# Weight sums of a paired feed-forward product made by accumulating DMAs from GpSimd, in a two-layer encoder trunk

## The reference, cut to what matters

```
for i in range(2):
    u = rms_norm(h, mix_norm_g[i])
    h = h + (conv_pool_mixer if i == 0 else gla_mixer)(u, ...)
    u = rms_norm(h, ffn_norm_g[i])
    a = relu(u @ ffn_w1[i])            # (528, 1024) @ (1024, 4096)
    h = h + (a * a) @ ffn_w2[i]        # (528, 4096) @ (4096, 1024)
return rms_norm(h[:, 16:], final_norm_g)
```

## Time and profile before

| | |
|---|---|
| median of 3 runs | 1162.88 us |
| profiled execution | 1161.42 us |
| its span | 1159.6 us |
| granted TensorE clock | 0.995 |
| TensorE busy | 1127.1 us, 97% |
| VectorE busy | 753.5 us, 65% |
| ScalarE busy | 522.0 us, 45% |
| GpSimd busy | 2.3 us |
| HBM traffic | 99.1 MB, 85 GB/s over the span |

### The profile page before, as it was taken

The page is one execution under the profiler, slowest core; times in us unless marked ns, Lnnn a source line. Parts: engine busy times, 40 slices in busy tenths (PEclk is TensorE's granted clock), DMA queues, the critical chain, the costliest instruction groups (busy, mean ns, idle before and its releaser), DMA issues.

```text
span 1159.6 us, 19207 instructions
## 1 busy us (share of the span) xinstructions
PE 1127.1 (97%) x7817; PEld 1048.7 (90%) x7817; DVE 753.5 (65%) x1039; ACT 522.0 (45%) x802; POOL 2.3 (0%) x30
## 2 busy tenths in 40 slices
PE   6999999999999999999999999999989999999997
PEld 6999999999999999999999888787889899899886
DVE  5898897786686785454353345665786786785443
ACT  7436554454454444333443133543454444454332
POOL 0000000000000000000000000000000000000000
PEclk9999999999999999999899999999999999999999
DMA  6322022233233224222113211132224224224311
GB/s 200 109 73 73 2 73 73 73 109 110 74 105 114 72 76 141 87 96 73 56 56 109 73 45 64 38 109 73 73 73 146 73 76 142 72 81 136 109 37 73
DMA packets 98819, 100.10 MB, mean 86 GB/s; under 512 B 2786, under 2 KB 95644, under 8 KB 98748
## 3 DMA queue, kind: packets, MB, share of 16 engines
q1 hardware_dynamic: 98684, 99.02, 26.5%
q10 hardware_dynamic: 64, 0.07, 0.0%
HBM read 96.99 MB, written 2.10 MB: 85 GB/s over the span
## 4 chain that ended last, share of the span: by engine, by line
PE 86%; DVE 6%; ACT 4%; issue 2%; DMA 1%; SPq 0%; ACTq 0%; DVEq 0%
PE ps L1701 53%; PE ps L1888 19%; PE ps L1955 5%; PE ps L1817 3%; PE ps L1997 1%; PE ps L2012 1%; DVE relu L1359 1%; PE ps L1749 1%; PE ps L1709 1%; DVE w_lo L494 1%; DVE c_lo L1378 1%; DMA raw<-in_cp_w_in_dram 1%; ACT parts L879 1%; ACT w_hi L487 1%; DVE rstd L1155 1%
## 5 line engine op out<-in xcount | busy, mean ns | idle before, releaser
L1701 PE MATMUL ps<-u_lo,w_hi 128*128 128x272 f32 (+1 forms) x1120 | 298.9, 323 | 3.3 <-DVE u_lo L1197 3.3
L1701 PE MATMUL ps<-u_hi,w_hi 128*128 128x272 f32 (+1 forms) x1120 | 295.6, 319 | 0.0
L1701 PE MATMUL ps<-u_hi,w_lo 128*128 128x272 f32 (+1 forms) x1120 | 295.2, 319 | 0.0
L494 DVE TENSOR_TENSOR w_lo<-raw,w_hi 128x1024 fp32r<-128x1024 f32 x132 | 161.1, 1223 | 117.9 <-ACT w_hi L487 117.9
L487 ACT ACTIVATE w_hi<-raw 128x1024 fp32r<-128x1024 f32 x132 | 138.4, 1052 | 146.5 <-PE ps L1701 135.4
L1701 PEld LDWEIGHTS ps<-u_lo,w_hi 128*128 128x128 f32 x1120 | 183.8, 188 | 21.4 <-issue 6.3
L1888 PE MATMUL ps<-c_lo,w_hi 128*128 128x264 f32 (+1 forms) x672 | 190.5, 284 | 11.9 <-ACT ps L902 9.1
L1701 PEld LDWEIGHTS ps<-u_hi,w_hi 128*128 128x128 f32 x1120 | 184.6, 189 | 16.2 <-issue 1.2
L1701 PEld LDWEIGHTS ps<-u_hi,w_lo 128*128 128x128 f32 x1120 | 183.6, 188 | 15.3
L1888 PE MATMUL ps<-c_hi,w_lo 128*128 128x264 f32 (+1 forms) x672 | 189.9, 283 | 0.0
L1888 PE MATMUL ps<-c_hi,w_hi 128*128 128x264 f32 (+1 forms) x672 | 189.7, 282 | 0.0
(11 more groups left out here) (241 smaller groups left out, 1545.8 us busy)
## 6 DMA issues: line engine op xcount, KB each, us to landing
raw<-in_ffn_w_dram SPq DMA_DIRECT2D x64, 1024.0 KB, 5.4
raw<-in_gla_w_in_dram SPq DMA_DIRECT2D x12, 1024.0 KB, 5.3
raw<-in_cp_w_in_dram SPq DMA_DIRECT2D x8, 512.0 KB, 5.3
raw<-in_cp_w_out_dram SPq DMA_DIRECT2D x4, 1024.0 KB, 5.1
raw<-in_gla_w_out_dram SPq DMA_DIRECT2D x4, 1024.0 KB, 5.1
xin<-in_x_dram SPq DMA_DIRECT2D x4, 512.0 KB, 5.4
raw<-in_cp_w_in_dram SPq DMA_DIRECT2D x2, 1024.0 KB, 5.1
out_dram<-y_tok SPq DMA_DIRECT2D x4, 512.0 KB, 3.0
```

Source lines behind the costliest of these rows:

```text
L494: dve.tensor_tensor(w_view(w_lo, n), half_view(raw, n), w_view(w_hi, n).bitcast(F32), ALU.subtract).then_inc(w_lo_ready, 1)
L1701: last = mm(ps[:, n % NS, c:c + b - a], l, r[:, a - origin:b - origin], start=(k == 0 and i == 0), stop=(k == count - 1 and i == 2))
```

## The change

The sums of weights are no longer made by VectorE. For each pair SP loads four tiles of `s_sum` straight from `ffn_w2`, GpSimd adds three more quarters by accumulating DMAs, waits, and adds s1 into s2 and s4 by two more. ScalarE's `pair_hi` waits for the last of these. To have only additions, all signs are positive: S1 = A21 + A22, S2 = A11 + S1, S3 = A11 + A21, S4 = A11 + A12 + S1; T1 is E1 - E2, the others change sign to suit, the kept copy of y is taken times -1, and the second row of outputs is subtracted from `h`.

The order in steps `i` changes: the weight group of an even step 4 or 6 comes behind the parts E1 to T1; the parts T2 to O2 are split in two (T2 alone, then O1 and O2), which makes four part groups per step pair instead of three; and pair 0's seed copy stands between them in step 7. The hardware loop is gone: all three blocks are written out, and `it` with it.

```diff
+        def w2_unit(layer, fb, p, m, k):
+            w2 = ffn_w2[layer].rearrange("(k p) n -> p k n", p=P)
+            at = 2 * P * p + P * m
+            return w2[:, fb * KD + k:(fb + 1) * KD:2, at:at + P]
 @ pair_hi
             if g in (1, 2):
-                act.wait_ge(s_ready, 4 * pair_number(layer, fb, p) + g + 2 + 16 * it)
+                act.wait_ge(sum_ready, 32 * (pair_number(layer, fb, p) + 1))
 @ sync
+            def load_sums(layer, fb, p):
+                b = pair_raw(layer, fb, p)
+                if p:
+                    sp.wait_ge(w_lo_ready, GROUPS[b - 1] + 3)
+                elif fb or layer:
+                    sp.wait_ge(w_lo_ready, GROUPS[pair_raw(layer, fb - 1, 3) if fb else pair_raw(0, PAIRED - 1, 3)] + 3)
+                for i, (m, k) in enumerate(((1, 0), (0, 0), (0, 0), (0, 0))):
+                    sp.dma_start(s_sum[:, i, :, :], w2_unit(layer, fb, p, m, k)).then_inc(sum_loaded, 16)
                     for j in range(4):
                         load(b + 4 + j, w2[:, fb * KD:(fb + 1) * KD, 256 * j:256 * (j + 1)])
+                        if fb < PAIRED:
+                            load_sums(layer, fb, j)
 @ gpsimd
+            def add_sums(layer, fb, p):
+                q = pair_number(layer, fb, p)
+                s1, s2, s3, s4 = (s_sum[:, i, :, :] for i in range(4))
+                pool.wait_ge(sum_loaded, 64 * (q + 1))
+                for dst, m, k in ((s1, 1, 1), (s4, 0, 1), (s3, 1, 0)):
+                    pool.dma_start(dst, w2_unit(layer, fb, p, m, k), accum_op=ALU.add).then_inc(sum_first, 16)
+                pool.wait_ge(sum_first, 48 * (q + 1))
+                for dst in (s2, s4):
+                    pool.dma_start(dst, s1, accum_op=ALU.add).then_inc(sum_ready, 16)
 @ scalar, step i
-                            pair_hi(layer, fb, 0, i - KD // 2, it)
-                        act.wait_ge(t_ready, 3 * count + 1 + 12 * it)
-                        act.activation(c_hi[:, E1:T1 + 1, j, 0:w], now[:, E1:T1 + 1, :], ACT.Copy)
+                        part_hi(E1, T1, 1)
+                        if i >= KD // 2:
+                            pair_hi(layer, fb, 0, i - KD // 2)
 ...
+                        part_hi(T2, T2, 2)
+                        if i == KD - 1:
+                            seed(0)
+                        part_hi(O1, O2, 2)
+                        part_hi(T3, T4, 3)
 @ vector, pair p
-                    if p < KD // 2 - 1:
-                        pair_sums(layer, fb, p + 1, it)
-                    dve.wait_ge(copied, 2 * q + 2 + 8 * it)
+                    dve.wait_ge(copied, 2 * q + 2)
 @ scalar, vector, tensor
-                paired_ffn(layer, 0, tokens)
-                with act.Fori(0, FBLK - 2) as it:
-                    paired_ffn(layer, 1, tokens, it)
+                for fb in range(PAIRED):
+                    paired_ffn(layer, fb, tokens)
```

More of the change, by code:

```diff
@@ L664, in _ @@
             last.then_inc(consts, 3)
+            def add_sums(layer, fb, p):
[7 more added lines that the diff above has]
+                    pool.dma_start(dst, s1, accum_op=ALU.add).then_inc(sum_ready, 16)
+            for layer in range(2):
+                for fb in range(PAIRED):
+                    for p in range(KD // 2):
+                        add_sums(layer, fb, p)
         @block.scalar
@@ L864, in paired_ffn, with part_hi @@
                     now = parts8[:, j % 2, :, 0:w]
-                    evacuated(act, n, it)
+                    evacuated(act, n)
                     src = relu[:, i % 2, a:b].rearrange("p (t n) -> p t n", t=2)
+                    def part_hi(first, last, t):
+                        act.wait_ge(t_ready, 3 * count + t)
+                        act.activation(c_hi[:, first:last + 1, j, 0:w], now[:, first:last + 1, :], ACT.Copy)\
+                           .then_inc(part_hi_ready, 1)
                     if i % 2 == 0:
@@ L876, in paired_ffn @@
[L876 to L877 removed]
+                            split_hi(block + i + 4)
+                        part_hi(E1, T1, 1)
+                        if i >= KD // 2:
+                            pair_hi(layer, fb, 0, i - KD // 2)
                     else:
                         act.activation(now[:, O1:O2 + 1, :], src, ACT.Square).then_inc(sq_ready, 1)
[L880 removed]
@@ L1392, in paired_ffn @@
                          .then_inc(t_ready, 1)
                         part_lo(E1, T1, 1)
-                    else:
-                        dve.wait_ge(sq_ready, t + 1 + 8 * it)
-                        V.tensor_tensor(now[:, T2, :], now[:, O2, :], now[:, T1, :], ALU.subtract)\
+                        if i >= KD // 2:
+                            pair_lo(layer, fb, 0, i - KD // 2)
+                    else:
+                        dve.wait_ge(sq_ready, t + 1)
+                        V.scalar_tensor_tensor(out=now[:, T2, :], in0=now[:, T1, :], scalar=-1.0,
+                                               in1=now[:, O2, :], op0=ALU.mult, op1=ALU.subtract)\
@@ L1397, in paired_ffn @@
                          .then_inc(t_ready, 1)
                         V.tensor_tensor(now[:, T3, :], now[:, O2, :], now[:, E2, :], ALU.subtract)
-                        dve.wait_ge(t_ready, 3 * count + 2 + 12 * it)
-                        V.tensor_tensor(now[:, T4, :], now[:, O1, :], now[:, T2, :], ALU.subtract)\
+                        part_lo(T2, T2, 2)
+                        dve.wait_ge(t_ready, 3 * count + 2)
+                        V.scalar_tensor_tensor(out=now[:, T4, :], in0=now[:, T2, :], scalar=-1.0,
+                                               in1=now[:, O1, :], op0=ALU.mult, op1=ALU.subtract)\
@@ L1432, in paired_ffn @@
                     next_lo(1)
[L1433 removed]
+                    dve.wait_ge(late_added, q + 1)
                     add_pair(0)
@@ L1459, in ffn_all @@
             def ffn_all(layer, tokens):
-                paired_ffn(layer, 0, tokens)
-                with dve.Fori(0, FBLK - 2) as it:
-                    paired_ffn(layer, 1, tokens, it)
+                for fb in range(PAIRED):
+                    paired_ffn(layer, fb, tokens)
                 ffn(layer, FBLK - 1, tokens)
@@ L1686, in parts, with exact @@
                 return ((0, *tokens),)
-            def exact(n, lhs, rhs, count, tokens, before=None, it=0, middle=None, at=KD // 2, origin=0):
-                start_slot(n, it)
+            def exact(n, lhs, rhs, count, tokens, before=None, middle=None, at=KD // 2, origin=0):
+                start_slot(n)
                 for k in range(count):
@@ L1922, in ffn_all @@
             def ffn_all(layer, tokens):
-                paired_ffn(layer, 0, tokens)
-                with pe.Fori(0, FBLK - 2) as it:
-                    paired_ffn(layer, 1, tokens, it)
+                for fb in range(PAIRED):
+                    paired_ffn(layer, fb, tokens)
                 ffn(layer, FBLK - 1, tokens)
```

176 lines of the change are left out of this document (77 added, 99 removed).

## The result

The changed kernel takes 1457.43 us (median of four, 1453.74 to 1461.82) against 1162.1 us: 1.2532 times as long, interval [1.2507, 1.2556]. The profiled execution has a span of 1460.0 us, 300.4 more than before. The forecast was 1370, range 1245 to 1545, slower with 0.95: the direction was right, and so was the mechanism in pairs 1 to 3; the size fell short by 87 us, and half of that stands in pair 0, where no wait was expected.

What follows compares the result with a forecast made beforehand. TensorE was taken to bound the kernel, busy 1127.1 of 1159.6 us. 1161.4 + 192 (transfer chain, boundary gain included) + 15 (clock) = 1368 us; with the median 1.5 us higher, 1370 was predicted, range 1245 to 1545.

Steps and rivals of the forecast that it cites:

- VectorE's sums are worth nothing in pairs 1 to 3: Paired blocks: removing the sums frees 65.8 us of VectorE, but no TensorE wait in pairs 1 to 3 hangs on them.
- Three transfers in a row: Each pair's sums: A + B + C = L against 6.1 us available; a pair takes the greater of 10.2 and L + 4.1.
- L = 18.5: Length in us of a pair's three dependent transfer stages, between 11.8 and 25.8; costs 32.0 us a block, 192 in all.
- A: First stage: SP's four 256 KB loads into s_sum until landed; between 4.4 and 9.3 us, taken as 7.
- C: Last stage: GpSimd's two accumulating copies of s1 into s2 and s4; between 3.4 and 6.6 us, taken as 4.5.
- B: Middle stage: GpSimd's three accumulating 256 KB loads; between 4.0 and 9.9 us, taken as 7.
- Pair 0 fits up to L = 20: Each block's first pair: its transfers are in time up to about 20 us; above, a block is 4L - 43.5 longer.
- The boundary order gains 1.7 us a block and T comes at 229.1: Pair 0: TensorE's waits fall from 2.62 to 0.9 us; T is the end of weight group 2's low half.
- The clock, 2.5 us a block: Behind pair 3: TensorE's gaps lower its clock, costing 0 to 3.5 us a block; 2.5 taken six times, 15 us.
- Short transfers: Rival: every stage takes its shortest likely landing, L = 12.8, total 1258 us, or about 1230 by the skill's fit; chance 0.11.
- GpSimd's issue as the bound: Rival: each of five accumulating transfers costs GpSimd 4.42 us to issue, L = 35.4, total about 1770 us; chance 0.12.
- A hidden chain: Rival: the transfers are hidden and only the boundary gain is left, 1153 us; chance 0.04.

Runs made afterwards that it cites:

- experiment 1: The changed kernel with only the transfers undone: VectorE makes the four sums again, all positive, the new order stays; 1158.39 us, 0.9960 of the kernel before.
- experiment 7: The changed kernel with plain copies instead of accumulates, all nine transfers of a pair issued by SP, same waits between stages; 1291.26 us.

## Why the prediction was right, and where it was short

*VectorE's sums are worth nothing in pairs 1 to 3.* Right: with them back (experiment 1) the only waits of TensorE in the paired product are the six of its list, all in pair 0.

*Three transfers in a row, started by the reuse of s_sum, longer than the 6.1 us there are; a pair takes L + 4.1.* Right for pairs 1 to 3, in start (0.03 us after T) and in law: four kernels with L from 14.1 to 21.0 us follow it within 0.3 us (table), and another buffer takes 144 us away.

*L = 18.5.* Short: 21.0. A was 7.1 (taken 7), C 4.7 (taken 4.5), B 9.3 where I took 7. So the term that was too small is B, the accumulates. That an accumulate reads its destination as well was in the sum; that its transfers come out as 44,928 packets where plain ones take 9,600, and that three issues on GpSimd take 3.9 us, was not. As plain copies B is 6.2, and from SP 4.9; of the 3.1 us between accumulates and plain copies the three issues give up to 1.7 (3.9 us against 2.2), and whether the rest comes of the packets is not shown. 2.5 us by three pairs by six blocks are 45 us.

*Pair 0 fits up to L = 20.* The limit was sound, its use was wrong: I put the same L there as in the other pairs, but its accumulates run beside a raw load, 27.4 us in the mean. By the limit itself it is then 7.4 us late. Measured against experiment 7, where pair 0 is in time, T comes 46 us later over the six blocks. This is the step that went wrong: by the forecast's own list of signs a gap in pair 0 speaks against it, and 31.7 of the 255 us that TensorE waits in the paired product stand there. Its own second formula, 4L - 43.5 for an L above 20, shows the price of the one figure for all places: with 27.4 for one of the four L and 21.0 for three it gives 46.9 us a block.

*The boundary order gains 1.7 us a block and T comes at 229.1.* Right where the transfers make the sums and pair 0 is in time: experiment 7 has T at 228.9 in the first block, and TensorE's wait there is 1.0 us (0.9 forecast). With VectorE's sums it was 4.5 us in all and nothing in the first block of either layer (experiment 1). The forecast also multiplied the first block's 2.6 us of waits by six; four of the six blocks had only 1.3 us to give.

*The clock, 2.5 us a block.* Right: 2.1 to 2.9, 14.9 in all where 15 was taken.

Together 207 + 45 + 46 = 298 us by this account; the span grew by 300.4, and the six paired products account for all of it (256.6 us before, 557.5 after). The medians grew by 295, and the changed kernel's four spans lie between 1451.9 and 1460.0 us, so that the sum comes out within 3 us is in part luck.

*The rivals.* Short transfers needed L below 13; even plain copies from SP have 14.1. The Trainium skill, "DMA: Bandwidth & Descriptors", section "Anatomy of one DMA", fits a GpSimd transfer as 2.0 us + bytes / 436e3; the estimate from it is 2.6 us for 256 KB. Here a plain one inside SBUF landed in 2.5 us in the median, which agrees, a plain one from HBM in 3.8 and an accumulating one from HBM in 6.8, so the measurement decides against taking it for accumulates. GpSimd's issue as the bound is out: 1.3 us each where that rival needed 4.42. A hidden chain is out.

## What to carry to other kernels

Work that nobody waited for gained nothing by being moved to the DMA queues. A chain of dependent transfers has to be held against the time from the release of its buffer to its first use, with the return path added: here 21 us against 6. Cost the accumulate apart from the copy, and cost each transfer with the others that are in flight at that place, not by one figure for all places. The cheap gain was elsewhere, in filling an engine's short waits for its neighbour with work that is due later: 13 us here.

## What the runs showed of the hardware that was not expected

- Accumulating transfers of 31.46 MB took 2.5 times the DMA engines' time of plain ones of the same shape from GpSimd (225 against 89 us) and 4.7 times the packets. An accumulate in SBUF of 256 KB landed in 3.9 us instead of 2.5, one from HBM in 6.8 instead of 3.8.
- GpSimd's issue of an accumulating transfer took 1.31 us (3.93 for three) from HBM and 0.89 in SBUF, with VectorE's work beside it (3.96 for three) or without; a plain one took 0.75 and 0.55, and SP issued the same sizes in 0.5 to 0.6.
- A 1 MB load issued in the midst of three accumulates lengthened their stage from 9.5 to 13.4 us in the mean of four blocks, more than the 3 us or so that the load takes by itself (an estimate: 1 MB at the 379 GB/s of the earlier trace rows). Beside plain copies from GpSimd it cost 1 us (6.2 to 7.2).
